# The first modulation of a transformer block in five shares instead of four: the last quarter as two shares of two channel groups, with the K projection's tiles placed earlier

## The chip, the cores and the metric

The kernel runs on one core of one Trainium2 chip. The metric is the device time of one execution in microseconds (us). Each kernel is timed in several runs, and medians are compared.

## What is computed

One block of a diffusion backbone: 256 latent tokens `x` and 256 context tokens `ctx`, both 2048 channels wide, in float32. What matters here is its very beginning:

```python
mod = silu(c) @ ada_w + ada_b              # ada_w is 2048 x 12288: shift1, scale1, gate1, shift2, scale2, gate2
mod_c = silu(c_ctx) @ ada_w + ada_b
h  = rms_norm(x, norm1_g) * (1 + sc1) + sh1
hc = rms_norm(ctx, norm1_g) * (1 + csc1) + csh1
proj = h @ w_in                            # q, k, v of two attention branches, and gates
proj_c = hc @ w_in
```

No projection can start before the shift and the scale of its channels are known, and these are sums over all 2048 rows of the first 4096 columns of `ada_w`, 33.6 MB. Two attention branches, their merge and a convolutional MLP follow; the change leaves them alone.

## The kernel before, in words

The 2048 channels are 16 **channel groups** `kc` of 128 (KC = 16). The **head** computes the first modulation and, at the same time, job 0, the first K projection (512 output columns), since both need all of `h`.

*Modulation units.* `ada_w`'s shift and scale columns are cut into QUARTERS = 4 quarters `q` of four channel groups (SHARE = 4). A unit `("ada", q, kc)` is one 128-row strip of `ada_w` by the 512 shift and the 512 scale columns of quarter `q`: 512 KB by one DMA of SP (L523) into one of the SLOTS = 8 slots of `raw`. `unit_ada` on PE (L1749) multiplies its four pieces of 256 columns by the two conditioning columns (`c_pair`), one piece each in rows 0, 32, 64 and 96 of a PSUM bank, summed over `kc`. SP issues unit n once PE is done with unit n - 8 (`ada1_used`).

*End of a quarter.* ACT copies the sums to `mod_rows` (L741), PE turns them into columns (`turn_mod`, L1736, two transposes), DVE makes gain and shift of the four groups (`modulation1`, L1172 to L1177). Then for each channel group: PE turns the normalized tokens (`turn_tokens`, L1725), ACT applies gain and shift (`modulate`, L749), DVE splits the result into a high and a low part `hT` (`split_modulated`, L1182 and L1184).

*K units.* Strip pair `s` of `w_in` (channel groups 2s and 2s + 1; s = 0 to 7; 512 KB) is loaded by SP into `ada_raw` (L531), split by ACT (`head_hi`, L675) and DVE (`head_lo`, L1132), and used by PE in four **tiles** (s, t), 128 output columns each: six matmuls per tile (L1757 to L1759, `head_k`). A tile needs `hT` of its two channel groups. Here "tile (s, t)" and "unit (q, kc)" are always meant so.

The order is written out by hand. `K_AFTER` says before which unit of quarters 1 to 3 SP issues a K load (before kc = 3 and kc = 10; strips 6 and 7 last). `K_TILES` says behind which unit PE runs each tile of strips 0 to 5. Behind the last unit (3, 15) stand tiles (5, 2) and (5, 3), with `turn_mod(3)` between them, and then all of strips 6 and 7. ACT and DVE go through the same steps in an order of their own: sums of a quarter, two channel groups, a K strip, two channel groups, a K strip.

When the last gain is ready, POOL starts to load the rest of `ada_w` into `ada_raw` (L592, `mod1_ready`), which DVE sums beside the later projections (L1197, L1201). Job 1 (`L1829` on), a Q projection, follows job 0 on PE; its strips are loaded by SP (L511) into the slots of `raw` that the last eight units leave.

Of the kernel before, what the change touches and what calls it, by code (L numbers as in the profile page):

```python
# [23 lines left out]
P = 128  # L24
# [2256 lines left out]
```

## Time and profile before

| | |
|---|---|
| median of 3 runs | 1738.75 us (1736.94 to 1738.83) |
| the profiled execution | 1738.52 us, its span 1736.8 us |
| PE busy in the span | 1684.4 us, 97% |
| job 0's last matmul ends, job 1 begins | 132.95 us |
| DMA in the head | 386 to 387 GB/s from 24 us to 120 us |

The span is the profiled part of an execution. Times of the trace are counted from its start. A row of the trace in order of time gives the start, the duration, engine, line and operation, how many of it stand in a row, and in brackets how long the engine stood idle before it and what ended that. One modulation unit shows as eight matmul records (x8), a pair of units in a row as x16.

### The profile page before, as it was taken

Reading aid. Unit: us, or ns where it says so; the run is one execution under the profiler, and the core shown is the slowest. Engines: PE = TensorE matmul, PEld = TensorE weight load, DVE = VectorE, ACT = ScalarE, POOL = GpSimd, SP = SyncE. Lnnn points to the kernel's source line nnn. Section 1 sums busy time; section 2 is a strip of 40 time slices with the busy share of each in tenths; the row PEclk is TensorE's granted clock in tenths of the full one; section 3 lists DMA queues with packets and bytes.
Section 4 is the critical chain, followed back from the end, with each engine's and each line's share of the span. In section 5 each row is a group of like instructions: output and inputs, shape, how many; then the busy total and the mean of one; then the engine's idle time right before and its main releaser. Section 6 shows DMA issues by size and latency. Waiting matters only on the chain.

```text
span 1736.8 us, 23807 instructions
## 1 busy us (share of the span) xinstructions
PE 1684.4 (97%) x8800; PEld 1377.5 (79%) x8800; DVE 1082.6 (62%) x1349; ACT 752.5 (43%) x960; POOL 108.7 (6%) x161
## 2 busy tenths in 40 slices
PE   4999999999999999999999899999999999999996
PEld 1468888888888678888888788888888888888885
DVE  1338777768786575554555666666666666655556
ACT  2233222623221565444444455555555555444444
POOL 0002222122121000000000000000000000000000
PEclk7999999999999999999999999999999999999998
DMA  9999888269795127666565566666666665565551
GB/s 354 387 386 335 305 292 284 76 233 326 238 316 195 51 79 262 192 187 191 191 241 189 152 182 187 188 191 185 191 192 185 191 191 185 192 193 193 194 192 63
DMA packets 161237, 371.53 MB, mean 214 GB/s; under 512 B 11607, under 2 KB 12359, under 8 KB 160022
## 3 DMA queue, kind: packets, MB, share of 16 engines
q1 hardware_dynamic: 139808, 291.98, 52.2%
q0 software_dynamic: 20144, 74.22, 12.5%
q10 hardware_dynamic: 1222, 4.47, 0.6%
q8 instruction: 41, 0.67, 0.2%
q14 instruction: 22, 0.18, 0.0%
HBM read 368.43 MB, written 2.21 MB: 213 GB/s over the span
## 4 chain that ended last, share of the span: by engine, by line
PE 92%; DMA 4%; DVE 2%; ACT 1%; issue 1%; SPq 0%; POOL 0%; ACTq 0%; DVEq 0%
PE ps L1833 21%; PE ps L1832 10%; PE ps L1842 10%; PE ps L1844 10%; PE ps L1843 10%; PE ps L2218 4%; PE ps L2219 4%; PE ps L2220 4%; DMA raw<-in_ada_w 4%; PE ps L1757 3%; PE ps L1758 3%; PE ps L1759 3%; PE ps L1829 1%; PE ps L1749 1%; PE ps L1911 1%; PE ps L1893 1%
## 5 line engine op out<-in xcount | busy, mean ns | idle before, releaser
L1127 DVE TENSOR_TENSOR w_lo<-raw,w_hi 128x1024 fp32r<-128x1024 f32 x480 | 584.7, 1224 | 431.7 <-ACT w_hi L669 431.2
L669 ACT CAST w_hi<-raw 128x1024 fp32r<-128x1024 f32 x480 | 503.4, 1050 | 771.4 <-PE ps L1844 273.8
L1833 PE MATMUL ps<-h2T,w_hi 128*128 128x512 f32 x1320 | 463.0, 394 | 0.0
L1832 PE MATMUL ps<-h2T,w_lo 128*128 128x256 f32 x1320 | 366.9, 278 | 0.0
L1833 PEld LDWEIGHTS ps<-h2T,w_hi 128*128 128x128 f32 x1320 | 247.9, 188 | 53.6
L1832 PEld LDWEIGHTS ps<-h2T,w_lo 128*128 128x128 f32 x1320 | 248.4, 188 | 4.2
L1842 PE MATMUL ps<-w_hi,hT 128*128 128x512 f32 x512 | 202.5, 395 | 0.0
L1201 DVE SCALAR_TENSOR_TENSOR ada_acc<-ada_raw,silu_c,ada_acc 128x512 f32<-128x512 f32 x240 | 180.0, 750 | 32.3 <-DMA ada_raw<-in_ada_w 16.9
L1844 PE MATMUL ps<-w_hi,hT 128*128 128x512 f32 x512 | 199.4, 390 | 0.0
L1843 PE MATMUL ps<-w_lo,hT 128*128 128x512 f32 x512 | 199.4, 389 | 0.0
L2218 PE MATMUL ps<-w_hi,f_hi 128*128 128x512 f32 x352 | 137.0, 389 | 1.0 <-DVE conv_in L1578 1.0
L2219 PE MATMUL ps<-w_lo,f_hi 128*128 128x512 f32 x352 | 136.9, 389 | 0.0
L2220 PE MATMUL ps<-w_hi,f_lo 128*128 128x512 f32 x352 | 136.9, 389 | 0.0
L592 POOL DMA_DIRECT2D ada_raw<-in_ada_w x128 | 91.3, 713 | 385.9 <-DVE ada_acc L1201 224.5
L1842 PEld LDWEIGHTS ps<-w_hi,hT 128*128 128x128 f32 x512 | 96.1, 188 | 22.0 <-issue 2.7
L1844 PEld LDWEIGHTS ps<-w_hi,hT 128*128 128x128 f32 x512 | 96.1, 188 | 20.3
L1843 PEld LDWEIGHTS ps<-w_lo,hT 128*128 128x128 f32 x512 | 96.2, 188 | 19.2
L1757 PE MATMUL ps<-hT,w_hi 128*128 128x512 f32 x256 | 103.7, 405 | 1.0 <-DVE hT L1184 1.0
L1758 PE MATMUL ps<-hT,w_hi 128*128 128x512 f32 x256 | 99.9, 390 | 0.0
L1759 PE MATMUL ps<-hT,w_lo 128*128 128x512 f32 x256 | 99.9, 390 | 0.0
L1833 PE MATMUL ps<-hT,w_hi 128*128 128x512 f32 x240 | 84.2, 393 | 0.0
L2218 PEld LDWEIGHTS ps<-w_hi,f_hi 128*128 128x128 f32 x352 | 66.1, 188 | 15.1 <-issue 1.3
(222 smaller groups left out, 1920.0 us busy)
## 6 DMA issues: line engine op xcount, KB each, us to landing
raw<-in_ffn_w_up SPq DMA_DIRECT2D x176, 512.0 KB, 3.8
raw<-in_w_in SPq DMA_DIRECT2D x152, 512.0 KB, 4.8
ada_raw<-in_ada_w POOLq DMA_DIRECT2D x128, 512.0 KB, 6.1
raw<-in_ffn_w_down SPq DMA_DIRECT2D x88, 512.0 KB, 4.2
raw<-in_ada_w SPq DMA_DIRECT2D x64, 512.0 KB, 10.6
raw<-in_w_out SPq DMA_DIRECT2D x32, 512.0 KB, 3.9
raw<-in_w_branch_a SPq DMA_DIRECT2D x16, 512.0 KB, 3.7
raw<-in_w_branch_b SPq DMA_DIRECT2D x16, 512.0 KB, 3.6
```

What stands on the lines that cost most here:

```text
L669: act.copy(w_hi[:, s % SPLIT_SLOTS, :], raw[:, s, :]).then_inc(hi_ready[s], 1)
L1127: dve.tensor_tensor(w_lo[:, s % SPLIT_SLOTS, :], raw[:, s, :], w_hi[:, s % SPLIT_SLOTS, :], ALU.subtract).then_inc(lo_ready[s], 1)
L1201: dve.scalar_tensor_tensor(acc, raw_columns, silu_c[:, kc:kc + 1], acc, ALU.mult, ALU.add).then_inc(ada_summed, 1)
L1757: pe.matmul(o, w_hi[:, row4(slot), at], hT[:, :, 0, kc, :], start=(kc == 0), stop=False)
L1832: pe.matmul(ps[:, b + t, 0:SEQ], w_lo[:, row4(s), at], high(kc), start=False, stop=False)
L1833: mm = pe.matmul(o, w_hi[:, row4(s), at], both(kc), start=False, stop=(kc == KC - 1))
L1842: pe.matmul(ps[:, b, :], hi, w_hi[:, row4(s), at], start=(kc == 0), stop=False)
L1843: pe.matmul(ps[:, b, :], hi, w_lo[:, row4(s), at], start=False, stop=False)
L1844: mm = pe.matmul(ps[:, b, :], lo, w_hi[:, row4(s), at], start=False, stop=(kc == last))
L2218: pe.matmul(ps[:, b, :], hi, w_hi[:, row4(s), at], start=start, stop=False)
L2219: pe.matmul(ps[:, b, :], hi, w_lo[:, row4(s), at], start=False, stop=False)
L2220: return pe.matmul(ps[:, b, :], lo, w_hi[:, row4(s), at], start=False, stop=stop)
```

## The change

The last quarter becomes two **shares** of two channel groups each: SHARES = (4, 4, 4, 2, 2). In a share of two groups a unit is two 128-row strips (2u and 2u + 1) by 256 shift and 256 scale columns: still 512 KB and still four pieces for PE, but two DMAs of 256 KB with rows of 1 KB in place of one with rows of 2 KB, and eight units per share. There are 48 + 16 = 64 units as before. PE's four pieces are now strip 2u's shift and scale and strip 2u + 1's, so the two strips' sums lie in different PSUM rows; `turn_mod` adds them as it turns them, with a matmul by `pair_sum` (made once by DVE from the identity) in place of a transpose. `turn_mod` and `modulation1` run five times instead of four.

`K_LOADS` and `K_TILES` are new tables: K loads stand before units (1, 2), (1, 8), (2, 3), (2, 9), (3, 1), (3, 4), (4, 3), and only strip 7 comes last. 26 tiles instead of 24 have a place behind a unit. ACT and DVE take a K strip after every second channel group. `turn_mod(q - 1)` stands right behind unit (q, 0).

```diff
-QUARTERS = 4
-SHARE = KC // QUARTERS
-K_AFTER = (3, 10)
-K_TILES = {(0, 0): (1, 6), (0, 1): (1, 8), (0, 2): (1, 10), (0, 3): (1, 12),
...
-           (5, 0): (3, 11), (5, 1): (3, 12), (5, 2): (3, 15), (5, 3): (3, 15)}
+SHARES = (4, 4, 4, 2, 2)
+FIRST_KC = [sum(SHARES[:q]) for q in range(len(SHARES))]
+ROWS_OF = [2 if n == 2 else 1 for n in SHARES]
+UNITS_OF = [KC // n for n in ROWS_OF]
+K_LOADS = {(1, 2): 0, (1, 8): 1, (2, 3): 2, (2, 9): 3, (3, 1): 4, (3, 4): 5, (4, 3): 6}
+K_TILES = {(0, 0): (1, 5), (0, 1): (1, 6), (0, 2): (1, 8), (0, 3): (1, 9),
...
+           (6, 0): (4, 5), (6, 1): (4, 6)}
...
-                    sp.dma_start(raw[:, n % SLOTS, :].rearrange("p (a n) -> p a n", a=2),
-                                 shift_scale[:, kc, :, GROUP * q:GROUP * (q + 1)]).then_inc(raw_landed[n % SLOTS], 16)
+                    cols = slice(P * FIRST_KC[q], P * (FIRST_KC[q] + SHARES[q]))
+                    dst = raw[:, n % SLOTS, :].rearrange("p (k a n) -> p k a n", k=ROWS_OF[q], a=2)
+                    for k in range(ROWS_OF[q]):
+                        sp.dma_start(dst[:, k, :, :], shift_scale[:, ROWS_OF[q] * u + k, :, cols])\
+                            .then_inc(raw_landed[n % SLOTS], 16)
...
+            dve.tensor_tensor(pair_sum[:], consts[0:PIECE_AT[-1] + 2, 0:PIECE_AT[1] + 2],
+                              consts[0:PIECE_AT[-1] + 2, PIECE_AT[2]:PIECE_AT[-1] + 2], ALU.add)\
+                .then_inc(vecs_ready, 1)
...
+                    if SHARES[q] == 4:
+                        mm = pe.transpose(ps[:, MOD_BANK, at:at + rows], columns, consts[0:rows, 0:rows])
+                    else:
+                        mm = pe.matmul(ps[:, MOD_BANK, at:at + PIECE_AT[1] + 2], columns, pair_sum[:],
+                                       start=True, stop=True)
...
-            turn_tokens(KC - 3)
-            for s in range(SLOTS - 2, SLOTS):
-                take(0, s)
...
+            head_k(SLOTS - 2, 2)
+            turn_mod(len(SHARES) - 1)
+            head_k(SLOTS - 2, 3)
+            turn_tokens(KC - 1)
+            take(0, SLOTS - 1)
```

**SP's queue, quarter 2 to the end of the head.** L523 is a unit's load before, L542 after (two rows of it, 128x2x256, make one unit in the new shares); L531 and L550 are K loads. Before:

```order
L523 DMA raw<-in_ada_w 128x2x512 x7
L531 DMA ada_raw<-in_w_in 128x2x512
L523 DMA raw<-in_ada_w 128x2x512 x9
L531 DMA ada_raw<-in_w_in 128x2x512
L523 DMA raw<-in_ada_w 128x2x512 x7
L531 DMA ada_raw<-in_w_in 128x2x512
L523 DMA raw<-in_ada_w 128x2x512 x6
L531 DMA ada_raw<-in_w_in 128x2x512 x2
```

After:

```order
L542 DMA raw<-in_ada_w 128x2x512 x6
L550 DMA ada_raw<-in_w_in 128x2x512
L542 DMA raw<-in_ada_w 128x2x512 x7
L542 DMA raw<-in_ada_w 128x2x256 x2
L550 DMA ada_raw<-in_w_in 128x2x512
L542 DMA raw<-in_ada_w 128x2x256 x6
L550 DMA ada_raw<-in_w_in 128x2x512
L542 DMA raw<-in_ada_w 128x2x256 x14
L550 DMA ada_raw<-in_w_in 128x2x512
L542 DMA raw<-in_ada_w 128x2x256 x10
L550 DMA ada_raw<-in_w_in 128x2x512
```

The sixth K load (s = 5) stands behind four of the new units, before unit (3, 4); before, it stood behind ten units of the last quarter. The seventh, which was behind all units, now stands before unit (4, 3).

**PE in the middle of the last quarter.** L1749 and L1778 are a unit (x4 for one, x8 for two), the six rows L1757 to L1759 and L1787 to L1789 a tile. Before, units (3, 10) and (3, 11) stand together between two tiles:

```order
L1749 MATMUL ps<-raw,c_pair 32x256 x8
L1757 MATMUL ps<-hT,w_hi 128x512
L1758 MATMUL ps<-hT,w_hi 128x512
L1759 MATMUL ps<-hT,w_lo 128x512
L1757 MATMUL ps<-hT,w_hi 128x512
L1758 MATMUL ps<-hT,w_hi 128x512
L1759 MATMUL ps<-hT,w_lo 128x512
L1749 MATMUL ps<-raw,c_pair 32x256 x4
```

After, each of the units from (3, 5) to (4, 6) has a tile behind it; here units (4, 4) and (4, 5):

```order
L1778 MATMUL ps<-raw,c_pair 32x256 x4
L1787 MATMUL ps<-hT,w_hi 128x512
L1788 MATMUL ps<-hT,w_hi 128x512
L1789 MATMUL ps<-hT,w_lo 128x512
L1787 MATMUL ps<-hT,w_hi 128x512
L1788 MATMUL ps<-hT,w_hi 128x512
L1789 MATMUL ps<-hT,w_lo 128x512
L1778 MATMUL ps<-raw,c_pair 32x256 x4
```

**PE behind the last unit.** L1725 and L1747 are a `turn_tokens`, L1736 and L1764 a `turn_mod`. Before, unit (3, 15):

```order
L1725 MATMUL ps<-consts,tokens 128x128 x4
L1749 MATMUL ps<-raw,c_pair 32x256 x4
L1757 MATMUL ps<-hT,w_hi 128x512
L1758 MATMUL ps<-hT,w_hi 128x512
L1759 MATMUL ps<-hT,w_lo 128x512
L1757 MATMUL ps<-hT,w_hi 128x512
L1758 MATMUL ps<-hT,w_hi 128x512
L1759 MATMUL ps<-hT,w_lo 128x512
L1736 MATMUL ps<-consts,mod_rows 128x98 x2
L1757 MATMUL ps<-hT,w_hi 128x512
```

After, unit (4, 7):

```order
L1747 MATMUL ps<-consts,tokens 128x128 x4
L1778 MATMUL ps<-raw,c_pair 32x256 x4
L1787 MATMUL ps<-hT,w_hi 128x512
L1788 MATMUL ps<-hT,w_hi 128x512
L1789 MATMUL ps<-hT,w_lo 128x512
L1787 MATMUL ps<-hT,w_hi 128x512
L1788 MATMUL ps<-hT,w_hi 128x512
L1789 MATMUL ps<-hT,w_lo 128x512
L1764 MATMUL ps<-pair_sum,mod_rows 128x34 x2
L1787 MATMUL ps<-hT,w_hi 128x512
```

The shape is the same: last unit, tile, `turn_mod`, tile, `turn_tokens`, wait for `hT`. What follows is 48 matmuls with two more `turn_tokens` before (strips 6 and 7), and 24 matmuls after (strip 7).

## Rows read from the trace of the kernel before

**Rows 1.** The page's head: span, and busy time of each engine.
```profile
span 1736.8 us, 23807 instructions
...
PE 1684.4 (97%) x8800; PEld 1377.5 (79%) x8800; DVE 1082.6 (62%) x1349; ACT 752.5 (43%) x960; POOL 108.7 (6%) x161
```

**Rows 2.** Stretches of the head and behind it: busy time, TensorE clock, DMA share, GB/s.
```profile
core 0: us, PE busy (x) PEld busy (x) DVE busy (x) ACT busy (x) POOL busy (x), PEclk, DMA share, GB/s
40.00:58.00 18.00, 13.96 (x122) 6.13 (x114) 6.99 (x13) 6.44 (x11) 0.00 (x0) 0.86 1.05 387
58.00:100.00 42.00, 41.35 (x332) 22.68 (x332) 11.20 (x22) 9.80 (x17) 0.00 (x0) 1.00 1.05 386
100.00:120.00 20.00, 19.99 (x150) 11.97 (x149) 5.34 (x11) 5.43 (x9) 1.09 (x2) 1.00 1.05 387
120.00:133.00 13.00, 11.99 (x57) 9.95 (x58) 9.52 (x15) 6.84 (x10) 2.37 (x4) 1.00 1.02 371
133.00:245.00 112.00, 112.00 (x578) 93.33 (x577) 88.24 (x106) 35.52 (x35) 29.28 (x42) 1.00 0.93 321
```

**Rows 3.** Waits of PE from 133 us to the end: the longest.
```profile
PE ps L2169 <- DVE x_normed L1533: 5.0, 4, 2.5
```

**Rows 4.** SP's issues of units (3, 5) and (3, 15), with time to landing.
```profile
L523 SPq DMA_DIRECT2D raw<-in_ada_w x1: 368/368/368, 87.9 to 87.9; - x1
...
DMA to landing us min/median/max: 10.9/10.9/10.9
...
L523 SPq DMA_DIRECT2D raw<-in_ada_w x1: 371/371/371, 105.3 to 105.3; - x1
...
DMA to landing us min/median/max: 8.6/8.6/8.6
```

**Rows 5.** PE in order of time: start, us, line, operation, idle before it.
```profile
82.33 0.64 PE L1749 MATMUL ps<-raw,c_pair 128*32 128x256 f32 x8 [0.65 <-DMA raw<-in_ada_w]
...
99.89 0.64 PE L1749 MATMUL ps<-raw,c_pair 128*32 128x256 f32 x8
...
101.96 0.60 PE L1725 MATMUL ps<-consts,tokens 128*128 128x128 f32 x4
102.49 0.64 PE L1749 MATMUL ps<-raw,c_pair 128*32 128x256 f32 x8
...
107.23 0.64 PE L1749 MATMUL ps<-raw,c_pair 128*32 128x256 f32 x8
...
109.41 1.07 PE L1749 MATMUL ps<-raw,c_pair 128*32 128x256 f32 x16
...
115.74 0.64 PE L1749 MATMUL ps<-raw,c_pair 128*32 128x256 f32 x8
...
117.80 0.33 PE L1736 MATMUL ps<-consts,mod_rows 98*128 98x98 f32 x2
...
121.00 0.47 PE L1757 MATMUL ps<-hT,w_hi 128*128 128x512 f32 x1 [1.02 <-DVE hT L1184]
...
127.51 0.39 PE L1757 MATMUL ps<-hT,w_hi 128*128 128x512 f32 x1
...
132.95 0.39 PE L1829 MATMUL ps<-hT,w_hi 128*128 128x512 f32 x1
```

**Rows 6.** DMA queue of SP, and its issues, from 60 to 100 us.
```profile
q1 hardware_dynamic: 7995, 15.40, 104.9%
...
raw<-in_ada_w SPq DMA_DIRECT2D x26, 512.0 KB, 10.5
```

**Rows 7.** DMA queue of ACT, 2.1 to 8.5 us: mostly rows of 512 bytes.
```profile
q10 hardware_dynamic: 420, 0.18, 10.0%
```

**Rows 8.** First modulation loads of POOL, and the first DVE step that reads one.
```profile
118.91 2.16 POOL L592 DMA_DIRECT2D ada_raw<-in_ada_w  x3 [111.66 <-DVE gain L1177]
...
130.76 0.48 DVE L1197 TENSOR_SCALAR ada_acc<-ada_raw,silu_c 128x512 f32<-128x512 f32 x1
...
ada_raw<-in_ada_w POOLq DMA_DIRECT2D x128, 512.0 KB, 6.1
```

More of the change, by code:

```diff
@@ L111, in loads_before, with units_until, landings @@
 def loads_before(j):
-    return len(ADA_UNITS) // SLOTS + j
+    return sum(ROWS_OF[q] for _, q, _ in ADA_UNITS) // SLOTS + j
+def units_until(q):
+    return sum(UNITS_OF[:q + 1])
+def landings(q, u):
+    return sum(ROWS_OF[n] * UNITS_OF[n] for n in range(q)) // SLOTS + ROWS_OF[q] * (u // SLOTS + 1)
 def turn_bank(kc):
@@ L258, in block_program @@
     mod_rows = place("mod_rows", att, [PIECE_AT[-1] + 2, 2, PIECE])
+    pair_sum = place("pair_sum", att + 4 * kb, [PIECE_AT[-1] + 2, PIECE_AT[1] + 2])
     x2 = place("x2", att, [P, TOK, D])
@@ L1721, in turn_tokens @@
                     pe.wait_ge(modulated_ready, 2 * (kc - 1))
-                if kc % SHARE == 1:
-                    pe.wait_ge(mod1_ready, kc // SHARE + 1)
+                if kc == FIRST_KC[SHARE_OF[kc]] + 1:
+                    pe.wait_ge(mod1_ready, SHARE_OF[kc] + 1)
                 for t in range(2 * TOK):
@@ L1784, in _ @@
             pe.transpose(ps[:, 2, 0:89], param_rows[0:89, 5, :], consts[0:89, 0:89]).then_inc(vecs_turned, 1)
-            for _, q, kc in ADA_UNITS:
-                unit_ada(q, kc)
-                if (q, kc) == (1, 1):
-                    turn_mod(0)
+            for _, q, u in ADA_UNITS:
+                unit_ada(q, u)
+                if q and u == 0:
+                    turn_mod(q - 1)
                 for (s, t), behind in K_TILES.items():
-                    if behind == (q, kc):
+                    if behind == (q, u):
                         if (s, t) == (0, 0):
@@ L1795, in _ @@
                         head_k(s, t)
-                        if (s, t) in ((1, 1), (3, 1), (5, 2)):
-                            turn_mod(q)
-                if kc == 14:
-                    turn_tokens(SHARE * q)
-                if q and kc in (2, 4, 5):
-                    turn_tokens(SHARE * (q - 1) + {2: 1, 4: 2, 5: 3}[kc])
-            turn_tokens(KC - 3)
-            for s in range(SLOTS - 2, SLOTS):
-                take(0, s)
-                for i in range(2):
-                    pe.wait_ge(hT_ready, 2 * s + i + 1)
-                    for t in range(TILES):
-                        mm = products_k(s, t, 0, 2 * s + i, i)
-                        if s == SLOTS - 2 and t == 1:
-                            turn_tokens(KC - 2 + i)
-                mm.then_inc(used[s], 1)
+                if u == UNITS_OF[q] - 2:
+                    turn_tokens(FIRST_KC[q])
+                if q:
+                    for n, behind in ((1, 2), (2, 4), (3, 5)):
+                        if u == behind and n < SHARES[q - 1]:
+                            turn_tokens(FIRST_KC[q - 1] + n)
+            head_k(SLOTS - 2, 2)
[3 more added lines that the diff above has]
+            take(0, SLOTS - 1)
+            for i in range(2):
+                pe.wait_ge(hT_ready, KC - 1 + i)
+                for t in range(TILES):
+                    mm = products_k(SLOTS - 1, t, 0, KC - 2 + i, i)
+            mm.then_inc(used[SLOTS - 1], 1)
             def sum_mod(g, j):
```

93 lines of the change are left out of this document (49 added, 44 removed), and 9 rows, old and new, of the table K_TILES.

## The prediction

> **What bounds the kernel now.** I read the page's head first: PE is busy 97% of the span [rows 1]. So a change pays only if it takes work off PE or fills a gap in it. The table of stretches says where gaps are [rows 2]: between 40 and 58 us PE is busy 13.96 us of 18, from 58 to 100 us 41.35 of 42, from 100 to 120 us 19.99 of 20, and between 133 and 245 us all of the time. The PE clock is granted in full (1.00, the 2.4 GHz level) from 58 us on. The view of waits adds that PE, from 133 us to the end, waits longest for a DVE step near the end of the block, 5.0 us in total [rows 3]; no row of that view names a DMA. What moves the end of job 0 (132.95 us) therefore moves the end of the kernel by as much.
>
> The head has a second bound almost as tight, the loads. Their rate is 386 to 387 GB/s in all stretches to 120 us [rows 2], which for 524,288 bytes is **one unit or K strip per 1.36 us**. So landing times can be counted: one place further back in SP's queue is 1.36 us later. Unit (3, 5) was issued at 87.9 us and took 10.9 us to land, so it was there at 98.8 us; unit (3, 15), at 105.3 and 8.6 us, at 113.9 us [rows 4]. PE in order of time [rows 5] took up (3, 5) at 99.89 us, 1.1 us after it landed, and (3, 15) at 115.74 us, 1.8 us after. The one wait for a load since 58 us that this view shows is 0.65 us, at 82.33 us. PE runs just behind the loads, and has its own work up to the end: from unit (3, 5) to the end of job 0 it takes 132.95 - 99.89 = 33.06 us, of which 1.02 us is one wait, at 121.00 us, for `hT` of the last quarter.
>
> **The change: where the loads hold PE.** The tables give PE tiles earlier in shares 1 and 2. That can fill the gaps of 40 to 58 us (18 - 13.96 = 4.0 us) and the 0.65 us. But by unit (3, 5) both versions have run the same tiles, strips 0 to 3, and tile (4, 0) stands behind (3, 5) in both. Whatever PE gains before, it cannot start (3, 5) before it has landed, and that comes later than before, for two reasons. K strip 5 now stands ahead of (3, 5) in SP's queue: one place, +1.36 us. And six units, (3, 0) to (3, 5), have rows of 1 KB. Their price is not in the trace; I bound it. In 40 us SP's queue moved 7995 packets (of 1926 bytes on average, the small completions included) in 104.9% of the time of 16 engines: 84.0 ns each [rows 6]. ACT's queue, mostly rows of 512 bytes, has 420 packets of 429 bytes on average in 10.0% of 6.4 us times 16: 24.4 ns each [rows 7]. A line through the two gives 45.7 ns for the 964 bytes that a 1 KB row averages with its completions. A unit has 17 packets per engine now and 34 then: 17 x 84.0 = 1428 ns against 34 x 45.7 = 1554 ns, and the same share above one, 1.049, makes that +0.12 us per unit. Lower bound: nothing, if bytes alone count. Upper bound: the price per byte of the short rows, 24.4 / 429 against 84.0 / 1926, 1.30 times as much, +0.42 us per unit. I take +0.12, which lies between the two rows on which it rests: +0.7 us for six units (0 to 2.5).
>
> So (3, 5) lands at 98.8 + 1.36 + 0.7 = 100.9 us, against the 99.89 us at which PE started it: **+1.0 us**. The gain from the tiles moved forward is waited away there.
>
> The Trainium skill ("DMA: Bandwidth & Descriptors", Why small descriptors are slow) gives a fixed overhead of about 3 cycles per packet beside one per 32 bytes. As an estimate by that page, a 2 KB row takes 67 cycles and two of 1 KB take 70, 4.5% or 0.06 us per unit more; the step would then be +0.7 us rather than +1.0. No run here shows rows of 1 KB yet.
>
> **The change: PE's work from (3, 5) on.** The same 11 units and 16 tiles follow as before, but laid out otherwise. Before, three pairs of units shared one switch; now each of ten units has a tile of its own. Pieces from the same view [rows 5]: a unit, a tile and a `turn_tokens` take 102.49 - 99.89 = 2.60 us; a unit and a tile take 109.41 - 107.23 = 2.18 us; a `turn_mod` 0.33 us; last unit to first matmul on the last `hT`, 121.00 - 115.74 = 5.26 us; 24 matmuls, 132.95 - 127.51 = 5.44 us. After the change:
> - (3, 5), (3, 6), (4, 2), (4, 6) with tile and `turn_tokens`: 4 x 2.60 = 10.40
> - (3, 7), (4, 1), (4, 3), (4, 4), (4, 5) with tile: 5 x 2.18 = 10.90
> - (4, 0) with the added `turn_mod` and tile: 2.51
> - the tail from (4, 7), of the same shape as before, with its wait of 1.02 us: 5.26
> - strip 7's 24 matmuls: 5.44
>
> The sum is 34.51 us against 33.06: **+1.45 us**. The shorter end (24 matmuls behind the wait instead of 48) is no gain in itself, since the tiles that left it run ahead of (4, 7), where PE has no gap either.
>
> **Edits at nothing.** SP issues two DMAs per unit, 2 x 0.37 us [rows 4], under the 1.36 us pace. PE reaches (4, 7) at 100.9 + 10.40 + 10.90 + 2.51 = 124.7 us; it has landed by 113.9 + 1.36 + 16 x 0.12 = 117.2 us (122.0 at the upper price), so the loads don't hold PE a second time, and K strip 6, ahead of it, has its cover too. If that cover were gone, the excess would count in full. `pair_sum` is one small DVE operation, at most the 0.48 us of a 128x512 step [rows 8], tens of us before its use. POOL's first load for the later modulation waits for the last gain and slips with (4, 7), from 118.9 by 8.9 us to 127.8 us [rows 8]; a median landing of 6.1 us makes 133.9, where DVE wants it at 130.8 + 2.4 = 133.2 us. The next split that PE needs stands behind it with some us to spare, so I count nothing.
>
> **Sum:** +1.0 + 1.45 = +2.4 us (+1.7 with free short rows) on the profiled execution's 1738.52 us: 1740.9, which is 1736.8 us of span and 1.7 us around it, shifted. The median shown is 0.23 us above that execution, so the forecast is **1741 us**, +0.13%. About 0.2%, 3.5 us, is what a measurement of this kernel can tell from no change.
>
> **Rivals.**
> - *Faster: the gaps are really filled.* If loads come early enough at (3, 5), by a shorter queue than I count, 4.0 + 0.65 us of gaps go and 1.45 stays: -3.2 us, 1735.3. If even the last landing set the end, it would be 117.2 + 5.26 + 5.44 = 127.9 us instead of 132.95: -5.0 us, 1733.5. For it: PE's gaps before 58 us are real. Against: the queue is full at one rate throughout [rows 2], and PE has no slack for ten tiles ahead of the last unit. 0.07.
> - *Slower: short rows are dear.* At +0.42 us per unit, (3, 5) lands at 98.8 + 1.36 + 2.5 = 102.7 us, +2.8, and the total is +4.2 us: 1742.7. It becomes slower by over 0.2% from about 0.3 us per unit on. For it: the 512-byte packets cost 1.30 times as much per byte. Against: rows of 1 KB lie nearer to 2 KB in that. 0.12.
> - *Slower: DVE waits for POOL's late loads and holds job 1's splits.* Should the loads take the 10 us of a full queue, not 6.1, DVE's first steps are some 4 us late and PE may stand up to 3 us: +5.4, 1743.9. It decides once the delay exceeds the splits' lead. Against: SP's queue is nearly empty then, since PE frees `raw` late. 0.06.
> - *Slower: small transfers don't overlap.* If a 256 KB transfer took the time of a 512 KB one, each new unit would cost 1.36 us more: the last lands at 113.9 + 1.36 + 21.8 = 137.0 us, job 0 ends at 147.7 us, +15 us, 1753.3. Against: 512 KB transfers, of which one alone took 10.5 us to land, follow each other every 1.36 us [rows 6]. 0.02. The Trainium skill ("DMA: Bandwidth & Descriptors", Bandwidth) speaks for this case: it advises transfers of 1 MiB and more, and counts about 2.0 us of fixed cost for each. The trace disagrees for a full queue: with that cost in series 512 KB would take 3.2 us as an estimate by the page, not 1.36.
>
> **How the numbers follow.** The forecast has the remaining 0.73. The range, 1737.5 to 1743.5 us, takes in the short rows from free (1740.2) to the upper bound (1742.7), part of the gaps filled, and a us of scatter; it leaves out the far rivals and half of the first. Faster by over 0.2%: most of the first rival, 0.05. Slower by over 0.2%: 0.12 + 0.02 + half of 0.06, and 0.01 of the forecast, 0.18. Within: 0.77.
>
> **What would show it.** In the new profile: PE waits for `raw` (or for tile (4, 0)) in 92 to 101 us and starts (3, 5) near 100.9 us; tiles of strips 2 and 3 stand earlier than before; no wait for loads between (3, 5) and (4, 7); (4, 7) starts near 124.7 us, long after landing; one wait of about 1 us for `hT` behind it; job 1 starts near 135.4 us; the rate stays near 387 GB/s to 110 us and falls behind it. I am wrong if job 1 starts before 133 us, if (3, 5) starts later than 102.7 us, or if a new wait appears behind 133 us.

## The result, and the profile after

The change is slower by about as much as a measurement can tell: median 1742.15 us (16 runs, 1740.5 to 1743.59) against 1738.74 us (16 runs, 1736.94 to 1740.48), ratio 1.002 with a 95% interval of 1.0013 to 1.0027. The forecast was 1741 us, the range 1737.5 to 1743.5. Job 1 starts at 136.09 us in the profiled execution, 3.14 us later than before, and the medians differ by 3.4 us: the head explains nearly all of the difference.

The page of the changed kernel begins as that of before does [rows 1], with 3.8 us more of PE busy time and 5.1 us more span:

```profile
span 1741.9 us, 23844 instructions
...
PE 1688.2 (97%) x8806; PEld 1379.6 (79%) x8806; DVE 1082.7 (62%) x1353; ACT 752.3 (43%) x961; POOL 108.7 (6%) x161
```

The stretches of the changed kernel, with the columns of [rows 2]:

```profile
40.00:58.00 18.00, 15.04 (x116) 7.45 (x112) 7.15 (x13) 6.33 (x11) 0.00 (x0) 0.81 1.05 387
58.00:100.00 42.00, 38.86 (x330) 21.68 (x322) 9.51 (x20) 9.65 (x17) 0.00 (x0) 1.00 1.06 378
100.00:120.00 20.00, 19.62 (x139) 12.00 (x132) 8.58 (x15) 6.39 (x12) 0.00 (x0) 1.00 1.09 359
120.00:133.00 13.00, 12.04 (x73) 8.25 (x72) 4.86 (x10) 5.68 (x9) 2.87 (x4) 1.00 0.78 271
133.00:245.00 112.00, 112.00 (x572) 93.73 (x571) 91.29 (x111) 35.70 (x35) 29.86 (x42) 1.00 0.95 331
```

Between 40 and 58 us PE did 1.1 us more, as the earlier tiles should make it. Between 58 and 100 us it was busy 2.5 us less (38.86 against 41.35): what was gained is lost again in waits before tile (4, 0). The rate is lower in the stretches in which loads have rows of 1 KB: 378 and 359 GB/s, where it was 386 and 387. What PE waits for from 58 to 137 us (total, times, longest):

```profile
PE ps L1778 <- DMA raw<-in_ada_w: 2.0, 3, 1.2
PE ps L1787 <- DVE w_lo L1148: 1.3, 1, 1.3
PE ps L1787 <- DVE hT L1205: 1.0, 1, 1.0
```

And PE of the changed kernel in order of time, with the columns of [rows 5] (L1764 is `turn_mod` by `pair_sum`, L1859 job 1):

```profile
76.09 0.47 PE L1787 MATMUL ps<-hT,w_hi 128*128 128x512 f32 x1 [1.27 <-DVE w_lo L1148]
...
95.35 0.64 PE L1778 MATMUL ps<-raw,c_pair 128*32 128x256 f32 x8 [0.50 <-DMA raw<-in_ada_w]
...
97.40 0.60 PE L1747 MATMUL ps<-consts,tokens 128*128 128x128 f32 x4
97.93 0.64 PE L1778 MATMUL ps<-raw,c_pair 128*32 128x256 f32 x8
99.74 0.64 PE L1778 MATMUL ps<-raw,c_pair 128*32 128x256 f32 x8 [1.17 <-DMA raw<-in_ada_w]
...
101.34 0.64 PE L1778 MATMUL ps<-raw,c_pair 128*32 128x256 f32 x8 [0.38 <-DMA raw<-in_ada_w]
101.91 0.50 PE L1787 MATMUL ps<-hT,w_hi 128*128 128x512 f32 x1
...
109.26 0.63 PE L1764 MATMUL ps<-pair_sum,mod_rows 98*128 98x34 f32 x4
...
125.09 0.64 PE L1778 MATMUL ps<-raw,c_pair 128*32 128x256 f32 x8
127.14 0.53 PE L1764 MATMUL ps<-pair_sum,mod_rows 98*128 98x34 f32 x4
...
130.53 0.47 PE L1787 MATMUL ps<-hT,w_hi 128*128 128x512 f32 x1 [0.96 <-DVE hT L1205]
```

Units (3, 2), (3, 4) and (3, 5) each wait for their landing: 2.05 us in all. (3, 5) starts at 101.34 us instead of 99.89, and tile (4, 0) behind it at 101.91 us instead of 100.46: **+1.45 us**. From tile (4, 0) to job 1 it is 34.18 us instead of 32.49: **+1.69 us**. The two make the 3.14 us.

The span grew by 2 us more than job 1's start. Most of that comes far behind the change. The first matmul of `df_values` (L1911, L1941) comes at 583.03 us before and 586.18 us after, still 3.15 us apart; the first transpose of `diff_o` (L2097, L2127) comes at 645.13 and 649.73 us, 4.60 us apart. The other 0.46 us come between 990 and 1490 us. In the stretch between the two marks, the differential attention, the granted clock differs. From 583 to 603 us, before, the changed kernel, and run e12 below (the same head but for two small operations):

```profile
583.00:603.00 20.00, 17.63 (x89) 11.00 (x88) 12.95 (x21) 12.03 (x30) 0.00 (x0) 0.91 0.19 54
```
```profile
583.00:603.00 20.00, 17.64 (x80) 11.49 (x80) 11.09 (x17) 10.72 (x24) 0.00 (x0) 0.85 0.26 79
```
```profile
583.00:603.00 20.00, 17.64 (x95) 11.22 (x93) 13.09 (x21) 12.76 (x30) 0.00 (x0) 1.00 0.25 77
```

The clock was 0.91, 0.85 and 1.00 there. In the fourteen traces of this case the stretch between the two marks takes 60.44 to 60.49 us where the clock from 583 to 603 us is 1.00 (e1, e3, e5, e12), 62.06 to 62.11 us where it is 0.91 (before and eight others), and 63.55 us in the changed kernel, at 0.85. Kernels of four and of five shares stand in both of the first two groups. With job 1 only 0.34 us earlier than in the changed kernel, e12's span is 1738.1 us, 3.8 us shorter. So one profiled span tells little here, and I compare job 1's start in the profile and medians.

### The profile page after: what moved, and what is told of

Same layout as the page of the kernel before. It is cut to its first block, busy times and chain, and to the rows that moved or that the text cites. A ratio compares the mean times of both kernels' runs of the same rounds, so it can differ in the third digit from the quotient of the medians.

```text
span 1741.9 us, 23844 instructions
## 1 busy us (share of the span) xinstructions
PE 1688.2 (97%) x8806; PEld 1379.6 (79%) x8806; DVE 1082.7 (62%) x1353; ACT 752.3 (43%) x961; POOL 108.7 (6%) x161
## 4 chain that ended last, share of the span: by engine, by line
PE 93%; DMA 3%; DVE 2%; ACT 1%; issue 1%; SPq 0%; DVEq 0%; POOL 0%; ACTq 0%
PE ps L1863 21%; PE ps L1862 10%; PE ps L1872 10%; PE ps L1874 10%; PE ps L1873 10%; PE ps L2248 4%; PE ps L2249 4%; PE ps L2250 4%; PE ps L1787 4%; PE ps L1789 3%; PE ps L1788 3%; DMA raw<-in_ada_w 3%; PE ps L1859 1%; PE ps L1778 1%; PE ps L1941 1%; PE ps L1923 1%
## 5 line engine op out<-in xcount | busy, mean ns | idle before, releaser
L1787 PE MATMUL ps<-hT,w_hi 128*128 128x512 f32 x256 | 103.8, 406 | 2.2 <-DVE w_lo L1148 1.3
L1789 PE MATMUL ps<-hT,w_lo 128*128 128x512 f32 x256 | 99.9, 390 | 0.0
```

What stands on the lines that cost most here:

```text
L1787: pe.matmul(o, w_hi[:, row4(slot), at], hT[:, :, 0, kc, :], start=(kc == 0), stop=False)
```

## The experiments

Twelve runs of eleven kernels follow (e11 is e7 again). All texts of expectation were on record before their run. In some of them times are counted from the x8 row of unit (1, 1), which waits for its landing in each kernel. That turned out a poor mark: it lies between 42.26 and 43.27 us in the changed kernel, e6 and e12, while tile (4, 0) starts at 101.91, 101.88 and 101.98 us in them. So the table counts from the span's start. Its columns: start of tile (4, 0); end of the split `w_lo` of K strip 4 on DVE, which this tile needs; from tile (4, 0) to job 1; job 1's start; the median and its ratio to before, run beside it on the same chip. The runs stood on three chips, where before had medians of 1738.77 us (e1 to e4), 1738.61 us (e5 to e8) and 1739.05 us (e9 to e12).

| | (4, 0) | split 4 | to job 1 | job 1 | median us | ratio, 95% |
|---|---|---|---|---|---|---|
| before | 100.46 | 100.08 | 32.49 | 132.95 | 1738.74 | |
| changed | 101.91 | 101.43 | 34.18 | 136.09 | 1742.15 | 1.0013 to 1.0027 |
| e1 tiles only | 100.97 | 100.83 | 32.48 | 133.45 | 1738.31 | 0.9990 to 1.0009 |
| e2 strip 5 back | 101.56 | 101.42 | 34.12 | 135.68 | 1740.06 | 1.0002 to 1.0021 |
| e3 2 KB rows, one DMA | 101.18 | 101.04 | 34.13 | 135.31 | 1741.01 | 1.0003 to 1.0022 |
| e4 2 KB rows, two DMAs | 101.92 | 101.77 | 34.11 | 136.03 | 1740.56 | 1.0003 to 1.0022 |
| e5 turn first | 100.20 | 98.81 | 32.49 | 132.69 | 1737.89 | 0.9986 to 1.0005 |
| e6 tiles in pairs | 101.88 | 101.74 | 32.91 | 134.79 | 1740.08 | 1.0000 to 1.0020 |
| e7 four, best | 100.36 | 99.98 | 30.65 | 131.01 | 1735.78 | 0.9976 to 0.9995 |
| e8 five, own tables | 99.67 | 99.53 | 34.16 | 133.83 | 1739.49 | 0.9993 to 1.0012 |
| e9 four edits, still five shares | 100.16 | 99.52 | 32.98 | 133.14 | 1739.29 | 0.9992 to 1.0010 |
| e10 e7 and e5 | 100.18 | 98.47 | 31.19 | 131.37 | 1736.72 | 0.9979 to 0.9997 |
| e11 e7 again | 100.67 | 100.29 | 30.78 | 131.45 | 1737.20 | 0.9980 to 0.9998 |
| e12 plain transposes | 101.98 | 101.55 | 33.77 | 135.75 | 1741.46 | 1.0005 to 1.0023 |

### e1: the earlier tiles alone

Four shares, loads as before; the tiles of strips 0 to 3 at the change's places, and `turn_mod` behind (q, 0) as there.

```diff
-K_TILES = {(0, 0): (1, 6), (0, 1): (1, 8), (0, 2): (1, 10), (0, 3): (1, 12),
...
-           (3, 0): (2, 13), (3, 1): (2, 15), (3, 2): (3, 1), (3, 3): (3, 3),
+K_TILES = {(0, 0): (1, 5), (0, 1): (1, 6), (0, 2): (1, 8), (0, 3): (1, 9),
...
+           (3, 0): (2, 11), (3, 1): (2, 13), (3, 2): (3, 0), (3, 3): (3, 2),
```

> Four shares and the loads as before; only the tiles of K strips 0 to 3 stand where the change puts them, and turn_mod stands behind unit (q, 0). Queue theory: PE fills its gaps before 58 us and is then held by the landing of unit (3, 5) at 98.8 us, which it starts at 98.8 to 99.0 us instead of 99.89; the rest, 33.06 us, is as before, so job 1 starts at 131.9 to 132.1 us instead of 132.95, and the time is 1 us under that of before. Rival, the gaps are gained in full: job 1 at about 129.8 us, 3 us faster. Rival, the early tiles themselves cost time: job 1 later than 133.5 us.

Job 1 came at 133.45 us, where 131.9 to 132.1 was expected: the tiles alone gain nothing. A wait took the gain that I had not on my list. PE of e1 in order of time:

```profile
96.80 0.60 PE L1725 MATMUL ps<-consts,tokens 128*128 128x128 f32 x4
97.33 1.07 PE L1749 MATMUL ps<-raw,c_pair 128*32 128x256 f32 x16
98.33 0.66 PE L1725 MATMUL ps<-consts,tokens 128*128 128x128 f32 x4
99.02 0.64 PE L1749 MATMUL ps<-raw,c_pair 128*32 128x256 f32 x8
100.97 0.47 PE L1757 MATMUL ps<-hT,w_hi 128*128 128x512 f32 x1 [1.31 <-DVE w_lo L1132]
```

(3, 5) was ready 0.9 us earlier than before (99.02 against 99.89 us), and tile (4, 0) behind it then waited 1.31 us for the split of strip 4. ACT and DVE of e1 show what that split waited for:

```profile
97.48 1.02 ACT L749 ACTIVATE modulated<-ps,shift,gain 128x256 f32<-128x256 f32 x2 [2.99 <-issue]
98.40 1.04 ACT L675 CAST w_hi<-ada_raw 128x1024 fp32r<-128x1024 f32 x1
```
```profile
98.54 0.43 DVE L1182 CAST hT<-modulated 128x512 fp32r<-128x512 f32 x1 [2.86 <-ACT modulated L749]
99.00 0.69 DVE L1184 TENSOR_TENSOR hT<-modulated,hT 128x512 fp32r<-128x512 f32 x1
99.61 1.22 DVE L1132 TENSOR_TENSOR w_lo<-ada_raw,w_hi 128x1024 fp32r<-128x1024 f32 x1
```

ACT and DVE, idle for almost 3 us, start when PE has turned the tokens of channel group 9 (the row at 96.80 us): modulate two channel groups' rows, then the strip. The profile names no releaser for ACT here ("issue"); that it is `turn_tokens` rests on the constant distance to it. From that row to the end of the split it is 4.03 us (96.80 to 100.83). In every kernel but e8, which loads strip 4 later, it is 4.02 to 4.09 us: before 95.99 to 100.08, changed 97.40 to 101.43, e5 94.73 to 98.81, e9 95.44 to 99.52. The change puts tile (3, 3) behind unit (3, 2), ahead of this `turn_tokens`, which costs a tile's 1.49 us; it comes 1.41 us later than before (97.40 against 95.99).

### e2: K strip 5 back behind the third share's units

```diff
-K_LOADS = {(1, 2): 0, (1, 8): 1, (2, 3): 2, (2, 9): 3, (3, 1): 4, (3, 4): 5, (4, 3): 6}
+K_LOADS = {(1, 2): 0, (1, 8): 1, (2, 3): 2, (2, 9): 3, (3, 1): 4, (4, 0): 5, (4, 3): 6}
```

> The change with one edit: K strip 5 is loaded before unit (4, 0) instead of before (3, 4), so one load fewer stands ahead of unit (3, 5). Queue theory: (3, 5) starts at about 100.0 us instead of 101.34, job 1 at 134.7 us instead of 136.09, 1.4 us faster than the change. Rival, the loss is PE's own work in the new layout (turn_mod, more switches) and the landing only takes up slack: job 1 stays at 136.1 us within 0.3.

The last rows of PE before tile (4, 0) in e2:

```profile
99.82 0.64 PE L1778 MATMUL ps<-raw,c_pair 128*32 128x256 f32 x8 [0.25 <-DMA raw<-in_ada_w]
...
101.56 0.47 PE L1787 MATMUL ps<-hT,w_hi 128*128 128x512 f32 x1 [1.10 <-DVE w_lo L1148]
```

Unit (3, 5) starts at 99.82 us instead of 101.34, 1.52 us earlier, where one place in the queue was counted at 1.36. The step stands. But tile (4, 0) gains 0.35 us only, and job 1 comes at 135.68 us instead of the expected 134.7; the split of strip 4 ends at 101.42 us, as in the changed kernel (101.43), and holds it for 1.10 us. In the changed kernel the two bounds lie 0.5 us apart: the load lets the tile go at 101.91, the split at 101.43 us.

### e3 and e4: rows of 2 KB in the last two shares

The units stay as they are, but read other weights, so that their rows are 2 KB: e3 in one DMA per unit, e4 in two.

```diff
-                    for k in range(ROWS_OF[q]):
-                        sp.dma_start(dst[:, k, :, :], shift_scale[:, ROWS_OF[q] * u + k, :, cols])\
-                            .then_inc(raw_landed[n % SLOTS], 16)
...
+                        row = 8 * (q - 3) + u
+                        sp.dma_start(raw[:, n % SLOTS, :].rearrange("p (a n) -> p a n", a=2),
+                                     shift_scale[:, row, :, GROUP * 3:GROUP * 4]).then_inc(raw_landed[n % SLOTS], 16)
```
```diff
-                        sp.dma_start(dst[:, k, :, :], shift_scale[:, ROWS_OF[q] * u + k, :, cols])\
-                            .then_inc(raw_landed[n % SLOTS], 16)
...
+                        for k in range(2):
+                            sp.dma_start(raw[:, n % SLOTS, GROUP * k:GROUP * (k + 1)],
+                                         shift_scale[:, row, k, GROUP * 3:GROUP * 4]).then_inc(raw_landed[n % SLOTS], 16)
```

> The change, but in the last two shares each unit is loaded by one DMA of 512 KB with rows of 2 KB, taken from the columns of the old last quarter: the sums of the last four channel groups are then of other weights, the work is the same. Queue theory with short rows at 0.12 to 0.19 us per unit: (3, 5) starts 0.7 to 1.1 us earlier than in the change, at 100.2 to 100.6 us, job 1 at 135.0 to 135.4 us, and the rate stays at 386 GB/s between 92 and 110 us instead of 355. Rival, short rows cost nothing and the rate fell because PE lagged: (3, 5) at 101.3, job 1 at 136.1 us.

> As the run before, but two DMAs of 256 KB per unit, each with rows of 2 KB (weights of the same strip, again not the right ones for the last four channel groups). If the length of the rows is what costs, this run is like the one before, (3, 5) at 100.2 to 100.6 us. If the size or the number of the transfers costs, it is like the change, (3, 5) at 101.3 us.

The stretch from 92 to 110 us: the changed kernel, e3, e4.

```profile
92.00:110.00 18.00, 15.89 (x125) 9.30 (x118) 7.23 (x14) 6.71 (x12) 0.00 (x0) 1.00 1.09 355
```
```profile
92.00:110.00 18.00, 16.67 (x129) 9.91 (x122) 7.55 (x16) 7.10 (x13) 0.00 (x0) 1.00 1.05 386
```
```profile
92.00:110.00 18.00, 16.78 (x137) 10.04 (x136) 7.17 (x15) 6.60 (x12) 0.00 (x0) 1.00 1.05 387
```

It is the length of the rows that costs, not the number or the size of the transfers: 355 GB/s with rows of 1 KB, 386 and 387 GB/s with rows of 2 KB, in transfers of 512 KB as of 256 KB. The units start earlier for it: (3, 5) at 100.36 and 100.26 us instead of 101.34. The cleanest measure is unit (3, 4), which waits for its landing in e3 as in the changed kernel: 98.99 against 99.74 us, 0.15 us for each of five units. PE of e3:

```profile
98.99 0.64 PE L1780 MATMUL ps<-raw,c_pair 128*32 128x256 f32 x8 [0.82 <-DMA raw<-in_ada_w]
...
100.36 0.64 PE L1780 MATMUL ps<-raw,c_pair 128*32 128x256 f32 x8
101.18 0.47 PE L1789 MATMUL ps<-hT,w_hi 128*128 128x512 f32 x1 [0.19 <-DVE w_lo L1150]
```

Again little of it arrives. In e3 tile (4, 0) is 0.73 us earlier, and waits 0.19 us for the split; in e4 PE came to the `turn_tokens` of group 9 at 97.75 us instead of 97.40, the split ended at 101.77 us, and the gain is nothing.

### e5: the earlier tiles with `turn_tokens` first

To test the cause found in e1: e1 with tile (3, 3) behind unit (3, 3) again, where `turn_tokens` stands ahead of it, and tiles (2, 0) and (2, 1) one unit later (they had a wait of the same kind at 76 us).

```diff
-           (2, 0): (2, 5), (2, 1): (2, 6), (2, 2): (2, 8), (2, 3): (2, 9),
-           (3, 0): (2, 11), (3, 1): (2, 13), (3, 2): (3, 0), (3, 3): (3, 2),
+           (2, 0): (2, 6), (2, 1): (2, 7), (2, 2): (2, 8), (2, 3): (2, 9),
+           (3, 0): (2, 11), (3, 1): (2, 13), (3, 2): (3, 0), (3, 3): (3, 3),
```

> As the run with the tiles alone (four shares, job 1 at 133.45 us), but tile (3, 3) stands behind unit (3, 3), so that turn_tokens(9) follows unit (3, 2) at once, and tiles (2, 0) and (2, 1) stand one unit later. Theory now: in that run tile (4, 0) waited 1.31 us for the split of K strip 4, which follows modulate(9) and so turn_tokens(9), held up by the tile put ahead of it. Then the wait goes, tile (4, 0) starts at 99.5 to 100.0 us instead of 100.97, job 1 at 132.0 to 132.5 us, the time is 0.5 to 1 us under that of before. Rival, strip 4 is late by its own load or by ACT: the wait stays, job 1 at 133.4 us.

Both waits for `w_lo` are gone, the split of strip 4 ends at 98.81 us, and PE in order of time shows what holds it now:

```profile
94.73 0.66 PE L1725 MATMUL ps<-consts,tokens 128*128 128x128 f32 x4
96.31 0.64 PE L1749 MATMUL ps<-raw,c_pair 128*32 128x256 f32 x8 [0.93 <-DMA raw<-in_ada_w]
```

Unit (3, 3) waits for its landing, at 96.31 us; in e9 and e10 it starts at 96.27 and 96.30 us. That is the loads' own time, and with it tile (4, 0) starts at 100.20 us, 0.26 us before that of the kernel before. Job 1 comes at 132.69 us, just behind the expected 132.0 to 132.5, and the interval of the ratio holds 1. So this order brings 0.3 us. It is not the bound on what earlier tiles can bring: PE stands for 0.93 us before (3, 3), and a tile directly behind `turn_tokens` might fill that. Since (3, 5) could start at 99.02 us in e1, 0.87 us before its time in [rows 5], I estimate at most 0.9 us from there. No run tried it.

### e6: five shares, tiles in pairs

```diff
-           (4, 0): (3, 5), (4, 1): (3, 6), (4, 2): (3, 7), (4, 3): (4, 0),
-           (5, 0): (4, 1), (5, 1): (4, 2), (5, 2): (4, 3), (5, 3): (4, 4),
-           (6, 0): (4, 5), (6, 1): (4, 6)}
+           (4, 0): (3, 5), (4, 1): (3, 6), (4, 2): (4, 0), (4, 3): (4, 0),
+           (5, 0): (4, 2), (5, 1): (4, 2), (5, 2): (4, 4), (5, 3): (4, 4),
+           (6, 0): (4, 6), (6, 1): (4, 6)}
```

> The change, but from tile (4, 2) on the tiles stand in pairs behind every second unit: six switches between modulation and K matmuls in place of ten; loads, work and the tables of shares 1 and 2 as in the change. Switch theory: each pair saves 2 x 2.18 - (1.00 + 1.40 + 1.58) = about 0.38 us, four pairs 1.5 us, less 0.2 us for turn_mod(3), which loses its cover: tile (4, 0) to job 1 takes 32.8 to 33.1 us instead of 34.18, job 1 starts at 134.8 us. Rival, the added time is turn_mod with its pair_sum alone: still 34.2 us and job 1 at 136.1 us.

From tile (4, 0) to job 1 it takes 32.91 us instead of 34.18, for the same units and tiles: four turns from units to tiles and back less bring 1.27 us, 0.32 us each (a net figure: `turn_mod` behind (4, 0) loses its cover by a tile in the same edit). One pair of units in e6, x16 in 1.07 us, where a single one of the changed kernel takes 0.64:

```profile
106.45 1.07 PE L1778 MATMUL ps<-raw,c_pair 128*32 128x256 f32 x16
107.58 0.63 PE L1764 MATMUL ps<-pair_sum,mod_rows 98*128 98x34 f32 x4
...
110.97 1.07 PE L1778 MATMUL ps<-raw,c_pair 128*32 128x256 f32 x16
```

### e7 and e11: four shares, the head's own gaps

If turns cost 0.32 us and the wait for `hT` behind the last unit 1 us, the kernel before has something to give. (4, 3) goes to (4, 2), (5, 0) to (5, 1)'s former place, and (5, 1) behind the last unit, so that `turn_mod(3)` stands between it and (5, 2) and two tiles cover `hT`.

```diff
-           (4, 0): (3, 5), (4, 1): (3, 6), (4, 2): (3, 8), (4, 3): (3, 9),
-           (5, 0): (3, 11), (5, 1): (3, 12), (5, 2): (3, 15), (5, 3): (3, 15)}
+           (4, 0): (3, 5), (4, 1): (3, 6), (4, 2): (3, 8), (4, 3): (3, 8),
+           (5, 0): (3, 12), (5, 1): (3, 15), (5, 2): (3, 15), (5, 3): (3, 15)}
...
-                        if (s, t) in ((1, 1), (3, 1), (5, 2)):
+                        if (s, t) in ((1, 1), (3, 1), (5, 1)):
```

> The kernel before with four tiles moved back: (4, 3) behind (3, 8) with (4, 2), (5, 0) behind (3, 12), and (5, 1), (5, 2), (5, 3) behind the last unit, two of them behind turn_mod(3). Theory: one tile more covers the wait of 1.02 us for hT, two switches fewer save 0.7 us, and PE is then held by the last landing, 113.9 us, instead of being 1.8 us behind it: job 1 at 131.4 to 131.8 us instead of 132.95, 1.2 to 1.5 us faster. Rival, the wait moves to the next channel group: job 1 at 132.6 us or later.

> The best version so far once more, for a second interval and beside the run with the earlier tiles: 1735.8 us, ratio 0.9986; job 1 at 88.4 after the x8 row of unit (1, 1).

It beats both kernels, by a little: 1735.78 us, ratio 0.9986 (0.9976 to 0.9995), and again 1737.20 us, 0.9989 (0.9980 to 0.9998). From tile (4, 0) to job 1 it takes 30.65 and 30.78 us instead of 32.49. The wait of 1.02 us is gone and two turns fewer make 0.64 us by e6's price, which is 1.66 of the 1.84 us; the edits were not run apart. PE's last stretch in e7 shows no wait:

```profile
108.51 1.93 PE L1749 MATMUL ps<-raw,c_pair 128*32 128x256 f32 x32
...
113.68 0.64 PE L1749 MATMUL ps<-raw,c_pair 128*32 128x256 f32 x8
...
115.74 0.33 PE L1736 MATMUL ps<-consts,mod_rows 98*128 98x98 f32 x2
...
131.01 0.39 PE L1829 MATMUL ps<-hT,w_hi 128*128 128x512 f32 x1
```

Unit (3, 15) starts at 113.68 us, 2.06 us before its time in [rows 5], and that is its landing: issued at 105.2, landed 8.4 us later.

### e8: five shares with tables of their own

```diff
-K_LOADS = {(1, 2): 0, (1, 8): 1, (2, 3): 2, (2, 9): 3, (3, 1): 4, (3, 4): 5, (4, 3): 6}
+K_LOADS = {(1, 1): 0, (1, 12): 1, (2, 2): 2, (2, 8): 3, (3, 4): 4, (3, 7): 5, (4, 2): 6}
...
+           (3, 0): (2, 10), (3, 1): (2, 11), (3, 2): (2, 11), (3, 3): (3, 3),
+           (4, 0): (3, 4), (4, 1): (3, 5), (4, 2): (3, 6), (4, 3): (3, 7),
+           (5, 0): (3, 7), (5, 1): (4, 2), (5, 2): (4, 4), (5, 3): (4, 4),
+           (6, 0): (4, 4), (6, 1): (4, 6)}
```

> Five shares with tables of their own making: fewer switches (tiles in pairs or threes), turn_tokens(9) right behind its unit, K strip 5 loaded before (3, 7) and strip 4 before (3, 4). Theory: with the three losses of the change removed (landing of (3, 5), late split of strip 4, switches) the shorter tail of two-group shares may count, job 1 at 131.3 to 132.5 us, faster than before by about 1 us, if short rows don't hold PE at (3, 3) to (3, 5). Rival, two-group shares cost more (1.1 us of short rows, 0.7 us of turn_mod) than they can give: job 1 at 133 us or later.

The rival came true: job 1 at 133.83 us, median 1739.49 us, 2.3 us earlier than in the change, level with before within the interval, and behind e7 by 2.8 us at job 1 and 3.7 us in the median. A better table of five shares may exist; this one was the only one tried.

### e9: four edits undone, the five shares kept

The changed kernel with the edits of e2, e3 (not shown again), e5 and e6. The tiles of strips 0 and 1 keep the change's places.

```diff
-K_LOADS = {(1, 2): 0, (1, 8): 1, (2, 3): 2, (2, 9): 3, (3, 1): 4, (3, 4): 5, (4, 3): 6}
+K_LOADS = {(1, 2): 0, (1, 8): 1, (2, 3): 2, (2, 9): 3, (3, 1): 4, (4, 0): 5, (4, 3): 6}
...
+           (2, 0): (2, 6), (2, 1): (2, 7), (2, 2): (2, 8), (2, 3): (2, 9),
+           (3, 0): (2, 11), (3, 1): (2, 13), (3, 2): (3, 0), (3, 3): (3, 3),
...
+           (5, 0): (4, 2), (5, 1): (4, 2), (5, 2): (4, 4), (5, 3): (4, 4),
+           (6, 0): (4, 6), (6, 1): (4, 6)}
```

> The changed kernel with four things undone at once: K strip 5 loaded before unit (4, 0) again, tile (3, 3) behind (3, 3) and tiles (2, 0), (2, 1) behind (2, 6), (2, 7), so that turn_tokens comes first, one 512 KB transfer with 2 KB rows per unit of the last two shares (other weights, so the last four groups' sums are of wrong columns), and the tiles from (4, 2) on in pairs. It stays in five shares. Theory (what holds PE at tile (4, 0) is K strip 5, the short rows and the split of strip 4; from there on it is the switches, and the rest is turn_mod by pair_sum): counted from the x8 row of unit (1, 1), tile (4, 0) starts at 57.1 (as with the tiles alone and turn_tokens first) instead of 59.65, takes 32.9 us to job 1 as with pairs alone, so job 1 starts at 90.0, 3.8 us ahead of the changed kernel (93.83) and 0.5 ahead of the kernel before (90.50); time 1738.3, ratio about 1.000. Rival (some cost of the two-group shares is still unnamed, e.g. the split of strip 5 arriving late again): job 1 at 91.5 or later, time over 1739.3.

Tile (4, 0) at 100.16 us and 32.98 us to job 1: the parts add up (e5's start of 100.20 and e6's 32.91 were to make 133.1; it is 133.14). The time, 1739.29 us, is before's within the interval, where 1738.3 was expected. What is left against the kernel before is 0.5 us behind tile (4, 0), about the price that e12 gives to `pair_sum`.

### e10: e7 with e5's earlier tiles

```diff
...
-           (2, 0): (2, 6), (2, 1): (2, 8), (2, 2): (2, 10), (2, 3): (2, 12),
-           (3, 0): (2, 13), (3, 1): (2, 15), (3, 2): (3, 1), (3, 3): (3, 3),
+           (2, 0): (2, 6), (2, 1): (2, 7), (2, 2): (2, 8), (2, 3): (2, 9),
+           (3, 0): (2, 11), (3, 1): (2, 13), (3, 2): (3, 0), (3, 3): (3, 3),
```

> Four shares of four groups: the tables of the best version so far (tile (5, 0) at (3, 12), tiles (5, 1) to (5, 3) behind the last unit) and ahead of (3, 5) the earlier tiles with turn_tokens first. Theory (PE at tile (4, 0) gains 0.95 us, as in the run with turn_tokens first, and the end keeps its 30.65 us from there): job 1 at 87.7 after the x8 row of unit (1, 1), 0.7 ahead of the best version (88.40), time about 1735.0. Rival (the last landing, unit (3, 15) at about 113.9, already sets the end in the best version, so that what PE gains before is waited away there): job 1 at 88.4 again and a longer wait for raw at the last unit, time 1735.8.

The rival holds: job 1 is 0.08 us ahead of e11, not 0.7. The last unit starts at 114.01 us (e11 beside it: 114.09), issued at 105.1 and landed 8.9 us later (105.5 and 8.5), and job 1 follows 17.36 us behind it in both. The two times, 1736.72 and 1737.20 us, don't differ beyond their scatter.

### e12: `turn_mod` with plain transposes

```diff
-                    if SHARES[q] == 4:
+                    if SHARES[q] > 0:
                         mm = pe.transpose(ps[:, MOD_BANK, at:at + rows], columns, consts[0:rows, 0:rows])
```

> The changed kernel with plain transposes in turn_mod for the last two shares, in place of the matmuls by pair_sum (the two strips' sums are not added, so the last four groups' gain and shift lack half of their sum). Theory (the two-group turn_mod costs 0.35 us twice more than a transposing one, because a float32 matmul is run in more passes): rows of turn_mod are x2, 0.12 us in total idle-free, job 1 starts 0.7 us earlier after tile (4, 0): 33.5 us instead of 34.18, time 1741.5. Rival (the price is the switch and the wait for mod_rows, not the form of the operation): 34.1 to 34.2 us, time 1742.1.

Unit (4, 0) with its `turn_mod`, and the next unit, PE of e12 in order of time:

```profile
108.78 0.64 PE L1778 MATMUL ps<-raw,c_pair 128*32 128x256 f32 x8
109.35 0.39 PE L1762 MATMUL ps<-consts,mod_rows 98*128 98x98 f32 x2
...
111.09 0.64 PE L1778 MATMUL ps<-raw,c_pair 128*32 128x256 f32 x8
```

Unit, `turn_mod` and tile take 2.31 us here (108.78 to 111.09) and 2.60 in the changed kernel (108.69 to 111.29). From tile (4, 0) to job 1, with both `turn_mod` in it, the form is worth 0.41 us (33.77 instead of 34.18), between what theory (0.7) and rival (0) said.

## Why the prediction was right, step by step

**What bounds the kernel, and that job 1's start carries over: right.** Over the fourteen rows of the table job 1 starts between 131.0 and 136.1 us and the medians go from 1735.8 to 1742.2 us with it; a line through them rises by 0.98 us per us, and no median lies more than 1.0 us off it. The list of PE's waits behind 133 us is the same, with the 5.0 us of [rows 3] at its top.

**The landing of (3, 5): right, 0.4 us too small.** Predicted 100.9 us, +1.0; the unit started at 101.34 us, +1.45. K strip 5's place is confirmed by e2 (1.52 us for 1.36). Short rows cost somewhat more than +0.12 us: in e2, without strip 5's place, the unit lands at 99.8, 1.0 us after the 98.8 of [rows 4], for six units, 0.17 us each; unit (3, 4) of e3 gives 0.15 us each; and e3 starts (3, 5) 0.98 us earlier than the change, 0.16 us each, with PE itself behind the landing. The line through two queues was a fair guess, the size a little low. One sign in the prediction was wrong, and did not fit its own sum: the rate was to stay near 387 GB/s to 110 us, while +0.12 us on 1.36 makes 354. It was 355 between 92 and 110 us. The estimate from the Trainium skill's page ("DMA: Bandwidth & Descriptors", Why small descriptors are slow), 0.06 us, was lower still. The Trainium skill's advice on the same page to batch transfers to 1 MiB and more (Bandwidth), given there with figures for transfers issued from GpSimd, was not needed in this full queue of SP: e4 moved 256 KB transfers at 387 GB/s.

**"The gain from the tiles moved forward is waited away there": right, for half of the reason.** The three waits for `raw` are there. But I named the landing as the only thing that holds tile (4, 0). Directly behind it stands the split of strip 4, which the change itself delays. In the changed kernel it decides nothing, since the landing is later still; in e1, e2 and e4 it does, and by 0.19 us in e3. The 1.27 us at 76.09 us is the same thing two strips earlier; it was not predicted, and cost nothing that was not waited away later.

**PE's work from (3, 5) on: right, 0.24 us too small.** Predicted 34.51 us, measured 34.75. The pieces of 2.60 and 2.18 us fit (101.34 to 125.09 us is 23.75, predicted 23.81). The term that was mis-sized is the tail: `turn_mod` by `pair_sum` costs 0.2 us more there than the transposes that I took it for (e12: 3.66 us from (4, 7) to the next `turn_tokens`, 3.88 in the changed kernel), and the last 24 matmuls took 5.56 us for 5.44. By experiments the +1.69 us divide into 1.27 for the turns between units and tiles (e6 has as many as before) and 0.41 for `pair_sum` (e12), 1.68 in all; the two were not undone together.

**Edits at nothing: right in what they came to, wrong in one figure.** (4, 7) started at 125.09 us (predicted 124.7) with no wait for a load since (3, 5); the wait for `hT` behind it is 0.96 us. POOL's first load came at 128.44 us (127.8), DVE's first step on it at 134.05 us, and PE has no new wait. But SP's issues did not take 0.37 us:

```profile
L542 SPq DMA_DIRECT2D raw<-in_ada_w x14: 563/669/1215, 90.6 to 101.2; - x14
```

Seven units took 11.69 us from the first issue to the end of the last, 1.67 us each, which is no longer under the pace of 1.36. No run of its own excludes that the issues set the pace. Against it stand the DMA engines, as full from 92 to 110 us as ever (a share of 1.09, 1.05 before), and e4, where the issues of the same number of DMAs with rows of 2 KB took 0.43 us in the median. Job 1 was to start at 135.4 us and started at 136.09.

**The rivals.** "The gaps are really filled", by 4.65 us, is refuted: even with strip 5 back, long rows and `turn_tokens` first (e9), PE gains 0.3 us at tile (4, 0), and by the estimate in e5 no order would gain more than about 0.9. Short rows "dear", at 0.42 us a unit, did not come (0.16), though the total came near to that rival's 1742.7 us. POOL's late loads and transfers that don't overlap did not show.

The sum of 1741 us missed the median by 1.2 us; 0.7 of it is the two terms above (0.44 for the landing, 0.24 for PE's work), the rest is within the scatter of the runs. The chance of 0.77 stood for "within 0.2%", of 0.18 for "slower"; the ratio lies on the line between the two.

## What to carry to other kernels

Where loads and the matrix engine run neck and neck, work that is moved forward pays only up to the next landing, and one place in a full queue is a fixed price (here 1.36 us per 512 KB). Before an engine's order is rewritten, look for the short operation in it that feeds the others (here a `turn_tokens` of 0.6 us, on which a chain of 4.03 us hangs): it should go ahead of long work, not behind. And count the turns between kinds of matmuls: here each cost 0.32 us, and taking some out, with the last wait covered by two tiles, gave the 0.1% by which e7 beats the kernel before.

## What the hardware showed that I had not expected

- Rows of 1 KB in a full queue: 355 GB/s in 256 KB transfers. Rows of 2 KB: 387 GB/s in 256 KB transfers (e4) and 386 in 512 KB transfers (e3). Two transfers of 256 KB with 2 KB rows cost no more than one of 512 KB.
- A float32 matmul by `pair_sum`, 98x34, shows as two records where a transpose of 98x98 shows as one (x4 and x2 for a `turn_mod`), and costs about 0.2 us more per `turn_mod` (0.41 us over two) although its output is a third.
- The granted clock in the differential attention stretch, far behind the change, differed between executions (0.91, 0.85, 1.00), and the spans of the changed kernel and e12 by 3.8 us, 3.5 more than their heads. Of these, 3.1 us arise in the stretch whose length follows that clock in all fourteen traces (60.5, 62.1 or 63.6 us). What sets the clock there was not tried.
